# Part of the context's feed-forward in front of the turns of four experts, and another order of work in the route, in a mixed two-block kernel

## The reference, cut to what matters

```python
for e in range(N_EXPERTS):
    hid = jax.nn.silu(t @ w_gate[e]) * (t @ w_up[e])
    y = y + combine[:, e:e + 1] * (hid @ w_down[e])
```

```python
x_ctx = xs + 0.5 * gate * swiglu(modulate(xs, g, shift, scale), w_gate, w_up, w_down)
```

## Time and profile before

| | us |
|---|---|
| median of 3 runs | 2151.0 |
| lowest, highest | 2147.88, 2154.74 |
| the profiled execution, its time | 2155.93 |
| the profiled execution, its span | 2154.1 |
| TensorE busy in the span | 2017.8 (94%) |
| VectorE, ScalarE busy | 1274.1 (59%), 884.9 (41%) |

### The profile page before, as it was taken

One profiled execution on the slowest core, in us unless ns is written; L12 is line 12 of the kernel. 1 busy time (PEld: TensorE's weight loads), 2 busy tenths in 40 slices (PEclk: granted clock), 3 DMA queues, 4 the chain that ended last, 5 costly groups with the idle time before them and its releaser, 6 DMA issues. The chain is left out here.

```text
span 2154.1 us, 32221 instructions
## 1 busy us (share of the span) xinstructions
PE 2017.8 (94%) x13104; PEld 1612.7 (75%) x13104; DVE 1274.1 (59%) x2027; ACT 884.9 (41%) x1438; POOL 58.1 (3%) x72
## 2 busy tenths in 40 slices
PE   7999999889998898788999999999999999999998
PEld 6897888654444666657888878668888888888887
DVE  5878545462112333335777763677777777877776
ACT  4434444211011222224655442475445554545444
POOL 1000000000000000000000030000001000100000
PEclk9999999989999999999999999999999999999999
DMA  9998984459999999999536453034446464374441
GB/s 351 402 401 339 393 314 157 156 239 396 421 421 417 405 407 410 416 409 378 199 118 235 176 157 117 10 118 157 167 135 227 156 225 154 128 231 163 141 151 40
DMA packets 211166, 540.73 MB, mean 251 GB/s; under 512 B 8894, under 2 KB 105752, under 8 KB 186440
## 3 DMA queue, kind: packets, MB, share of 16 engines
q1 hardware_dynamic: 208264, 531.69, 65.6%
q0 software_dynamic: 2192, 6.57, 1.1%
q10 hardware_dynamic: 560, 0.38, 0.1%
HBM read 537.56 MB, written 1.05 MB: 250 GB/s over the span
## 5 line engine op out<-in xcount | busy, mean ns | idle before, releaser
L1307 PE MATMUL lo<-xs,wp 128*128 128x512 f32 (+1 forms) x3392 | 591.7, 336 | 9.1 <-DVE wp L2682 5.8
L1307 PEld LDWEIGHTS lo<-xs,wp 128*128 128x128 f32 x3392 | 513.1, 189 | 87.1 <-issue 13.2
L987 ACT ACTIVATE wp<-ring 128x1024 fp32r<-128x1024 f32 (+2 forms) x432 | 347.5, 828 | 251.8 <-PE hi L1307 140.6
L2682 DVE TENSOR_TENSOR wp<-ring,wp 128x1024 fp32r<-128x1024 f32 (+2 forms) x432 | 397.8, 941 | 7.1 <-ACT wp L987 7.0
L1307 PE MATMUL hi<-hs,wp 128*128 128x256 f32 (+1 forms) x1842 | 316.3, 333 | 4.5 <-DVE hs L3034 3.2
L1307 PEld LDWEIGHTS hi<-hs,wp 128*128 128x128 f32 x1842 | 274.5, 189 | 43.0 <-DVE hs L3034 3.5
L1307 PE MATMUL lo<-ring,scratch 128*64 128x512 f32 (+1 forms) x1536 | 253.4, 594 | 16.0 <-DMA ring<-in_moe_w_up_dram 8.0
L1307 PEld LDWEIGHTS lo<-ring,scratch 128*64 128x64 f32 (+1 forms) x1536 | 79.7, 123 | 175.4 <-issue 162.9
L2689 DVE TENSOR_TENSOR ring_r<-ring,home 128x1024 fp32r<-128x1024 f32 x52 | 63.0, 1223 | 132.5 <-ACT home L995 132.5
L995 ACT ACTIVATE home<-ring 128x1024 fp32r<-128x1024 f32 x52 | 53.9, 1053 | 185.8 <-DMA ring<-in_ffn_w_down_dram 56.6
L1307 PE MATMUL hi<-xs,home 128*128 128x256 f32 x576 | 109.3, 294 | 14.3 <-DVE ring_r L2689 11.9
(11 more groups left out here) (493 smaller groups left out, 2761.0 us busy)
## 6 DMA issues: line engine op xcount, KB each, us to landing
ring<-in_mod_w_dram SPq DMA_DIRECT2D x72, 1024.0 KB, 14.7
ring<-in_moe_w_gate_dram SPq DMA_DIRECT2D x64, 1024.0 KB, 12.5
ring<-in_moe_w_up_dram SPq DMA_DIRECT2D x64, 1024.0 KB, 15.9
ring<-in_moe_w_down_dram SPq DMA_DIRECT2D x64, 1024.0 KB, 15.2
ring<-in_ffn_w_gate_dram SPq DMA_DIRECT2D x55, 1024.0 KB, 6.1
ring<-in_ffn_w_up_dram SPq DMA_DIRECT2D x55, 1024.0 KB, 8.6
ring<-in_ffn_w_down_dram SPq DMA_DIRECT2D x50, 1024.0 KB, 11.0
ring<-in_w_in_dram SPq DMA_DIRECT2D x20, 1024.0 KB, 13.3
```

The source lines that it names most:

```text
L987: act.activation(wp[:, q % SLOTS, 0, k:k + w.shape[1], :], w, ACT.Copy).then_inc(piece_hi, 2 // len(parts))
L1307: return pe.matmul(dst, lhsT, rhs, start=start, stop=stop, **kw)
L2682: tt(wp[:, q % SLOTS, 1, k:k + w.shape[1], :], w, wp[:, q % SLOTS, 0, k:k + w.shape[1], :].bitcast(F32), ALU.subtract).then_inc(piece_lo, ...
```

## The change

- **Route, ScalarE:** the two exponentials stand ahead of the context's copy and squares. The root of the context's rows moves into turn 0, behind the first SiLU.
- **Route, TensorE:** the filler matmuls (`keep_busy`) and the context's mean leave the route; counts are also made with the experts on the partitions. The order comes as a product: a one-hot of each expert's rank, times its number, summed over 32 partitions. The places and weights are transposed and permuted by products as well. The gather of turn 0 is cut in two halves with the order's sum between them. The turn of the last modulation, the permutation and the context's mean are in turn 0, around its up products.
- **Route, VectorE:** ranks from one comparison with a per-partition key over 32 elements; the work on modulation and context (`context_rows`) moves to turn 1.
- **One unit ahead:** the first half of turn 1's gate weights has a buffer of its own (`ahead`), so its load waits only for the order.
- **Front block:** the twelve pieces of tiles 0 to 3 with their three slices stand in front of turn 8, in the loads and on all engines. Each turn of four then carries the block of tiles one further on: turn 8 has tiles 4 to 7, turn 10 tiles 12 to 15. Turn 11 carries only the four gate pieces of tiles 16 to 19; their up slice is loaded behind its last expert unit and its four pieces (52 to 55) follow the turn.
- **Behind the turns:** tiles 20 and 21 are left. The transposes of x stand behind the gate piece of tile 20, the sum of squares behind that of tile 21, the root behind both tiles, and VectorE's reciprocal and the scaling of x's rows at the down pieces 0 to 3.

```diff
-EARLY_TILES = 18
-EARLY_PIECES = 52
-U_QUADS = U_MOE + 6 * PAIRS
-U_FFN[0] = U_QUADS + 15 * QUADS
-U_FFN[1] = U_FFN[0] + 5
+EARLY_TILES = 20
+EARLY_PIECES = 56
+U_QUADS = U_MOE + 6 * PAIRS + 2
+U_FFN[0] = U_QUADS + 15 * QUADS - 1
+U_FFN[1] = U_FFN[0] + 3
+
+
+def u_slice(u, b):
+    if u == 0:
+        return U_QUADS - 3 + b
+    return U_QUADS + 15 * (u - 1) + (0, 13 if u == QUADS else 5, 10)[b]
+
...
+                            if n is None:
+                                for e in range(2):
+                                    sp.dma_start(view(n, e), expert_of(w, bass.ds(experts[e], 1))[:, 0:k]).then_inc(ahead_loaded, 16)
+                                continue
...
+                if i == PAIRS:
+                    slice_units(0, range(3))
+                    overfull_units()
                 expert_units(i, [sp.value_load(order[0:1, at + e:at + e + 1], min_val=0, max_val=EXPERTS - 1) for e in range(experts_in(i))])
-            gate_up(up_unit(0, 16), (0, 0), 8)
-            gate_up(up_unit(0, 18), (0, 0), 9)
+            slice_units(QUADS, (1,))
...
-            act.wait_ge(fm_turned, 1)
-            act.activation(cT, hi[:, :, :], ACT.Copy).then_inc(fm_copied, 1)
-            act.wait_ge(fm_copied, 1)
-            act.activation(u0, cT, ACT.Square).then_inc(rms_sq, 1)
-            mod_copied(17)
-            act.wait_ge(rms_ms, 3)
-            act.activation(rstd_c, hi[:, 0, 0:T], ACT.Sqrt, bias=eps[:], scale=P / D).then_inc(rms_std, 1)
-            mod_cols(17)
             act.wait_ge(act_in, 1)
             act.activation(part(4200, TT, GROUPS), part(4192, TT, GROUPS), ACT.Exp).then_inc(act_out, 1)
             act.wait_ge(act_in, 2)
             act.activation(small[:, 34:36], small[:, 32:34], ACT.Exp).then_inc(act_out, 1)
+            act.wait_ge(fm_turned, 1)
+            act.activation(cT, hi[:, :, :], ACT.Copy).then_inc(fm_copied, 1)
+            mod_copied(17)
+            act.wait_ge(fm_copied, 1)
+            act.activation(u0, cT, ACT.Square).then_inc(rms_sq, 1)
+            act.wait_ge(rt_mm, 4)
+            act.activation(turned_by, in_columns, ACT.Copy).then_inc(act_out, 1)
+            mod_cols(17)
...
+                if i == 0:
+                    act.wait_ge(rms_ms, 3)
+                    act.activation(rstd_c, hi[:, 0, 0:T], ACT.Sqrt, bias=eps[:], scale=P / D).then_inc(rms_std, 1)
...
+            for q in range(12):
+                early_piece(q, True)
...
-                q = 12 * (i - PAIRS)
+                q = 12 * (i - PAIRS + 1)
...
+                if i == EX_TURNS - 1:
+                    expert_silu(i)
+                    expert_turned(i)
+                    early_round(q + 4)
+                    early_round(q + 5)
+                    expert_out(i)
+                    break
...
             mod_product(17)
-            pe.wait_ge(rms_sq, 3)
-            for c in range(KC):
-                ins = mm(hi[:, 0, 0:T], means[:, 1, :], u0[:, c, :], c == 0, c == KC - 1)
-            ins.then_inc(rms_ms, 1)
-            mod_turn(17)
-            keep_busy(hi[:, 1], 4)
+            pe.wait_ge(fm_copied, 1)
             pe.wait_ge(rt_comb, 1)
             ranks, counts = lo[:, 1, 0:TT * EXPERTS].rearrange("p (t n) -> p t n", t=TT), lo[:, 1, TT * EXPERTS:(TT + 1) * EXPERTS]
             mm(ranks[:, 0, :], before_me, chosen[:, 0, :])
             mm(ranks[:, 1, :], before_me, chosen[:, 1, :], True, False)
             mm(ranks[:, 1, :], means[:, 0, :], chosen[:, 0, :], False, True)
             for t in range(TT):
-                ins = mm(counts, means[:, 0, :], chosen[:, t, :], t == 0, t == 1)
+                mm(counts, means[:, 0, :], chosen[:, t, :], t == 0, t == 1)
+            for t in range(TT):
+                ins = mm(count_col, chosen[:, t, :], means[:, 0, 0:1], t == 0, t == 1)
             ins.then_inc(rt_mm, 1)
-
...
+            for t in range(TT):
+                pe.transpose(in_columns[:, TT + t, :], comb[:, t, :], ident)
...
-            gather()
+            gather(range(4))
+            pe.wait_ge(rt_comb, 2)
+            mm(order_row, means[0:EXPERTS, 0, :], numbered).then_inc(rt_mm, 1)
+            pe.wait_ge(md_copied, TURNS)
+            gather(range(4, KC))
+            for t in range(TT):
+                ins = pe.transpose(in_columns[:, t, :], place[:, t, 0:EXPERTS], ident)
+            pe.wait_ge(rt_comb, 3)
+            mm(rank_row, means[0:EXPERTS, 0, :], beneath).then_inc(rt_mm, 1)
...
+                if i == 0:
+                    mod_turn(17)
+                    pe.wait_ge(act_out, 3)
+                    for a in range(2 * TT):
+                        ins = mm(in_ranks[:, a, :], turned_by[:, a, :], picked)
+                    ins.then_inc(rt_mm, 1)
...
+                if i == 0:
+                    pe.wait_ge(rms_sq, 3)
+                    pe.wait_ge(rt_flag, 2)
+                    for c in range(KC):
+                        ins = mm(hi[:, 0, 0:T], means[:, 1, :], u0[:, c, :], c == 0, c == KC - 1)
+                    ins.then_inc(rms_ms, 1)
+                    pe.wait_ge(md_cols, TURNS)
...
+            for q in range(12):
+                early_piece(q)
...
-                q = 12 * (i - PAIRS)
+                q = 12 * (i - PAIRS + 1)
+                whole = i < EX_TURNS - 1
...
-                    early_piece(q + j)
+                    if whole:
+                        early_piece(q + j)
...
-                if tile == 18:
-                    pe.wait_ge(h_mul, tile)
-                    pe.wait_ge(xg_ready, TT)
-                    for t in range(TT):
+                    if (tile, a) == (20, 0):
+                        pe.wait_ge(h_mul, tile)
+                        pe.wait_ge(xg_ready, TT)
+                        for t in range(TT):
...
+                        ins.then_inc(fm_turned, 1)
+                    if (tile, a) == (21, 0):
+                        pe.wait_ge(rms_sq, 4)
                         for c in range(KC):
-                            ins = pe.transpose(hi[:, c // 2, (c % 2) * T + t * P:(c % 2) * T + t * P + P], x[:, t, c * P:c * P + P], ident)
-                    ins.then_inc(fm_turned, 1)
-                if tile == 19:
-                    pe.wait_ge(rms_sq, 4)
-                    for c in range(KC):
-                        ins = mm(hi[:, 0, 0:T], means[:, 1, :], un[:, c, :], c == 0, c == KC - 1)
-                    ins.then_inc(rms_ms, 1)
-            pe.wait_ge(rms_std, 4)
+                            ins = mm(lo[:, 0, 0:T], means[:, 1, :], un[:, c, :], c == 0, c == KC - 1)
+                        ins.then_inc(rms_ms, 1)
             for d in range(KC):
...
+            link(dve.tensor_reduce(rank_col, above, AX.X, ALU.add))
+            ts(numbered, first_numbers, rank_col, col_number, ALU.is_equal, ALU.mult).then_inc(rt_comb, 1)
+            ts(picked, first_numbers, rank_col, None, ALU.is_equal)
+            ts(beneath, key[0:EXPERTS], key_col, float(CW), ALU.is_lt, ALU.mult).then_inc(rt_comb, 1)
+            dve.tensor_copy(tallied, counts)
+            gathered_half(0, 0)
+            dve.wait_ge(rt_mm, 3)
+            dve.tensor_copy(order[:], order_row).then_inc(ex_order, 1)
+            gathered_half(0, 1)
+
...
-            for src, dst in ((place[:, :, 0:EXPERTS], place_by), (comb[:, :, :], comb_by)):
-                for t in range(TT):
-                    link(tt(masked, taken, by_expert(src[:, t]), ALU.mult))
-                    link(dve.tensor_reduce(dst[:, t], masked, AX.X, ALU.add))
...
+            dve.wait_ge(rt_mm, 5)
+            link(dve.tensor_copy(by_rank, in_ranks))
...
+                if i == 1:
+                    context_rows()
...
+            for q in range(12):
+                early_piece(q, True)
...
+                if i == EX_TURNS - 1:
+                    x_summed(i - 1, 1)
+                    expert_hidden(i)
+                    expert_back(i)
+                    early_rest(q + 4)
+                    early_rest(q + 5)
+                    expert_rest(i)
+                    break
...
-                if tile == 20:
-                    dve.wait_ge(rms_std, 4)
-                    link(dve.reciprocal(rstd_x, rstd_x))
-                if tile >= 20:
-                    for c in range(4 * (tile - 20), 4 * (tile - 19)):
-                        scaled(un[:, c], xT, c, mod_scale[:, 1], rstd_x)
...
+                if d == 0:
+                    dve.wait_ge(rms_std, 4)
+                    link(dve.reciprocal(rstd_x, rstd_x))
+                for c in (2 * d, 2 * d + 1):
+                    if c < KC:
+                        scaled(un[:, c], xT, c, mod_scale[:, 1], rstd_x)
```

More of the change, by code:

```diff
@@ L280, in down_units @@
             if f == 0:
-                return tuple(U_FFN[0] + 3 + j if p == 2 else U_QUADS + 15 * (2 * p + j) + 10 for j in range(2))
+                return tuple(U_FFN[0] + 1 + j if p == 2 else u_slice(2 * p + j, 2) for j in range(2))
             return tuple(U_FFN[f] + (5, 11, 15)[p] + j for j in range(2))
@@ L338, in early_weights @@
```

(32 more changed lines are left out.)

145 lines of the change are left out of this document (66 added, 79 removed).

## The result

| | before | after |
|---|---|---|
| median of 8 runs each, us | 2150.85 | 2159.62 |
| lowest to highest | 2146.72 to 2154.74 | 2157.79 to 2164.17 |
| profiled execution, its span | 2155.93, 2154.1 | 2159.77, 2157.9 |

The ratio is 1.0048 (95% 1.0036 to 1.0059): slower by 0.48%, 10.3 us by the ratio; the two medians lie 8.8 us apart. The time is inside the range of 2143 to 2162, but the forecast case (within 0.3% of before, 2147 to 2158) is not what happened; the slower side had 0.28.

A forecast was written before the change was run, and what follows sets the result against it. Loads bound the turns of four; the end follows TensorE's last awaited weights plus its remaining work. Terms -4.0 + 2.0 + 4.0 gave 2.0 us slower, 2153 from a median of 2151.0; range 2143 to 2162.

The forecast's parts named there:

- the forecast case: Whole kernel: lead spent in the block in front, end within 0.3% of before, 2147 to 2158 us; chance 0.55.
- the slower side: Whole kernel: slower than before by more than the 0.3% (6.5 us) the measurement can tell; chance 0.28.
- The route: Up to turn 0's down weights: exponentials first, warm gathers, shorter sort; experts start 12.0 us earlier, down weights reached 15.5 earlier.
- What the loads make of it: Turns of two experts: loads lead by 18 us, 2 of it from the own buffer; TensorE also 18 ahead.
- The block in front: Before turn 8: held ring slots leave three transfer gaps, 5.1, 9.6 and 7.1, in all 21.8 us; loads 4.0 late.
- The end of the stretch: Behind turn 11: up pieces start at 1004.2, but four pieces less remain; gain 4.0 us.
- What is given back: Tail: wait for x's rows costs 2.0 us, scaling of x's rows at the down pieces 4.0.
- The cold route: Rival: TensorE stays cold through both gathers, lead 12 not 18, 2159 us; chance 0.28, including longer front-block waits.
- The loads that catch up: Rival, expert loads: 4.6 us a unit, not 5.0, gives back 17 us over 43 units, 2136; chance 0.08.
- That the end costs nothing: Rival, tail: nothing is lost at the end and the lead is 21, so 2144 us; chance 0.07.
- slower units: Rival, front block: units at 5.9 us fill more of its 38 us, some 12 us of gaps, 2143; chance 0.02.

The follow-up runs named there:

- the two without the buffer: Changed kernel, and kernel before with only the route part, each without the own buffer for turn 1's first unit; ratios to before 1.0096 and 0.9943.
- the route-alone kernel: Kernel before with only the route part and the unit ahead, without front block, moved tiles or new tail: 2135.3 us, ratio 0.9938 to before.
- the block alone: Kernel before with front block, moved tiles and tail of the change, but old route and no unit ahead: ratio 1.0136 to before.

## Why the prediction came out as it did

**The route: right, 1.1 us too large.** ScalarE's exponentials no longer hold VectorE, both gathers run warm, and the experts start earlier, 11.8 us for 12.0. Of the 15.5 us, 14.4 came: what was put into turn 0 takes 1.05 + 1.07 + 3.72 = 5.8, not 4.7.

**What the loads make of it: right in kind, 2.5 us too large in this trace.** I gave the loads a lead of 18, of which 2 for the buffer. It is 15.5 in this trace and 16.2 on the mean of the six that share the code up to there; the two without the buffer have 13.4 and 13.6, where the prediction has 16. I let the loads lead by 2.5 us more than TensorE's own 15.5. Beyond TensorE's 14.4 they lead by 1.1 here, but by 2.2 or 2.3 in the other traces whose gathers are warm, so that step holds, and the route's 1.1 is the larger part of what is missing there.

**The block in front: the mechanism right, the three gaps 3.2 us short.** Three gaps of 5.1, 9.6 and 7.1 were forecast; 6.5, 11.2 and 7.3 are there, in the same order. The twelve pieces took 27.2 + 13.2 us and waits of 2.95 and 1.06, where I had 25.0 + 11.7, 2.9 and 1.0. In pieces 0 to 7 this size is partly chance: TensorE ran at half clock until 683, and the same eight pieces took 25.0 to 27.6 us in five other traces. Pieces 8 to 11 ran at a mean clock of 0.87 behind the wait of 2.95; my 11.7 was a warm group's time. Windows of after:

```profile
679.00:681.00 2.00, 2.00 (x11) 2.00 (x10) 0.00 (x0) 0.00 (x0) 0.00 (x0) 0.50 1.08 421
681.00:683.00 2.00, 2.00 (x11) 2.00 (x11) 0.00 (x0) 1.33 (x2) 0.00 (x0) 0.50 1.00 411
...
705.76:718.99 13.23, 13.23 (x96) 13.03 (x96) 6.30 (x9) 3.18 (x3) 0.00 (x0) 0.87 0.29 121
```

The block began 17.1 us early, not 18. So piece 15 freed its slot 4.7 us later than forecast (731.72 + 2.21 against 729.2), and that is most of the 5.9 us by which the first piece behind turn 11 came later than forecast (13.7 against 7.8); the last 1.2 I can't assign. The fourth gap, 2.4 us near 690, I did not see; with it the gaps are 5.6 us longer than my sum. The queue there stands in turn 8's gate units, in the slot of the first slice, which piece 3 frees. A like gap (174 GB/s from 688 to 692) is in the route-alone kernel too, where the stretch as a whole loses 1.5 us against before, so it belongs to the lead and not to the block.

**The end of the stretch: 1.2 us better than forecast.** Four pieces and two scatters took 13.9 us (1007.86 to 1021.78) where 15.1 stood in the sum.

**What is given back: 9.8 by the rows, 6.0 forecast.** The wait for x was 3.15, not 2.0, and the transposes behind it ran at clock 0.50, that is 1.2 GHz, 3.60 us against 1.91: 4.85 in all for a term of 2.0. The scaling at the down pieces was 4.0 forecast; down pieces and the wait behind them grew by 4.95, the scaling's part being 3.5. Where its start was put, 3.6 us behind TensorE's first down piece, 3.73 was measured.

**Sum.** +2.0 forecast, +11.1 in the trace, +10.3 in the times: 5.9 more than forecast ahead of the first piece behind turn 11, 3.2 more in the tail. The terms that were sized too small are the time that the front block holds its slots (the gaps) and what the tail gives back. That the time still lies in the range of 2143 to 2162 is in part luck: its upper side stood for a lead of 12 and a wait of up to 5.92 us at piece 8, and neither came.

**The rivals.** The cold route gave 2159 at a lead of 12 and decides below 13.5. The time is that, but the lead was 15.5 and its cause is refuted for this trace: the clock was 1.00 in both gathers. The loads that catch up (2136) did not; TensorE waits for them at 646 and 651. That the end costs nothing is refuted, and so are slower units: between the gaps the queue moved 389 to 423 GB/s, and 421 from 734 to 760. On the limit of about 358 GB/s for a core that the Trainium skill states (DMA: Bandwidth & Descriptors, Specifications), this trace again disagrees, with those 421 on the one core that ran. On the switch of ScalarE's tables (the Trainium skill, ScalarE: Activation LUTs, What ACT_TABLE_LOAD costs: 2.66 us) the row at 1045.57 shows 1.28, and VectorE's reciprocal starts 1.8 us behind the start of that row (1047.38), root included: less than the page's figure.

**The version that beats both** is the route alone with its buffer: 2135 us, 0.62% below before and 1.1% below the changed kernel. Without its buffer it is 0.57% below before, and the times can't tell the two apart. The changed kernel's tail, with the transposes one piece later, is worth its edit where the block in front is kept.

## What to carry to other kernels

Where loads set the time, work on the multiplier is free only as long as it frees the ring's slots at the rate of the queue; a block of pieces that holds three of six slots for some 40 us stops the queue, whatever lead the loads had (what follows came 29.6 us later without it, 29.5 with it). Count lost transfers (window length times one less the rate over its steady value), and do it for the whole stretch: on the trace after it gave 27.4 us in one line, where stepping through slots had given 21.8 beforehand. And take the common zero of two traces as late as the unchanged code allows: from the early product (414.15 and 410.30) the lead of the loads would read 13.9 us instead of 15.5. And before a sum is moved to an earlier place, look what its reader still has to do ahead of it: here the root waited for another row, and the earlier sum only took time from what came behind.

## What the runs showed that I had not expected

- Profiled executions with the same code differ ahead of all that was changed: an early modulation product starts between 408.92 and 416.76 us in ten traces, and from there to the end of the last one it is 21.8 to 21.9 us in four of them and 23.5 in six. Spans compared without a common zero would have been off by up to 7.8 us, and with an early one still by 1.6.
- TensorE's clock at the transposes of x was 0.50 after an idle time of 3.15 us and 1.00, 1.94 us for the same 16 transposes, after one of 0.27. The wait was paid for a second time, with 1.7 us.
- The distance from piece 8 of the front block to the first piece behind turn 11 was 302.1 to 302.8 us in the four traces with the buffer and whole front pieces, whose starts of piece 8 lie 2.2 us apart (303.0 with the block alone, 304.1 without the buffer): with the loads as the bound, the moment at which TensorE gives its slots back sets what follows.
